# 512-column products with halves added on VectorE in three more stages, and a reordered complex product, in a two-block fp32 model on one core

## The reference

```python
# first block
h = rms_norm(x, norm_ffn_pre)
x = x + rms_norm(conv_ffn(h, ffn_w_up, ffn_conv, ffn_w_down), norm_ffn_post)
# second block, mixer: y_b is the convolution branch
hy = centred_short_conv(hy, conv_w, conv_b)
x0, x1, v = jnp.split(hy, 3, axis=-1)
y_b = x0 * bidirectional_fftconv(v * x1, h_f, h_b, hyena_bias)   # spectrum of u times spectrum of the filter
# second block, experts (peer_ffn)
qh = (xb @ w_q)
s = jnp.einsum('thpc,hpnc->thpn', qh, sk)       # similarities to the sub-keys, then top-16 twice
act = jax.nn.gelu(jnp.einsum('td,thkd->thk', xb, u)) * g
out = jnp.einsum('thk,thkd->td', act, v)
```

## Time and profile before

| | |
|---|---|
| median of 3 runs | 1596.46 us (1592.6 to 1598.15) |
| the profiled execution | 1591.63 us |
| its span, first to last instruction | 1589.8 us |
| TensorE busy | 1551.2 us (98%) |
| GpSimd, VectorE, ScalarE busy | 1193.8, 996.0, 785.7 us |
| mean granted TensorE clock | 0.997 of full |

### The profile page before, as it was taken

The page is one execution under the profiler, slowest core; times in us unless marked ns, Lnnn a source line. Parts: engine busy times, 40 slices in busy tenths (PEclk is TensorE's granted clock), DMA queues, the critical chain, the costliest instruction groups (busy, mean ns, idle before and its releaser), DMA issues.

```text
span 1589.8 us, 30453 instructions
## 1 busy us (share of the span) xinstructions
PE 1551.2 (98%) x11198; PEld 1389.7 (87%) x11198; DVE 996.0 (63%) x1344; ACT 785.7 (49%) x1050; POOL 1193.8 (75%) x499
## 2 busy tenths in 40 slices
PE   7999999999999999999999999999999999999998
PEld 5688899997999889989999999888888888888886
DVE  5545477665220957743159962688888999954444
ACT  5456644556555555444544454454544444444443
POOL 6643689795887964568768998777777777789895
PEclk9999999999999999999999999999999999999999
DMA  8433466555555533336645555555555555566663
GB/s 279 165 111 108 151 219 185 185 184 160 185 184 158 164 113 101 118 124 183 218 144 184 183 180 178 172 167 163 164 167 159 171 160 168 165 221 192 192 194 121
DMA packets 72774, 267.90 MB, mean 169 GB/s; under 512 B 8176, under 2 KB 8448, under 8 KB 71744
## 3 DMA queue, kind: packets, MB, share of 16 engines
q1 hardware_dynamic: 70272, 253.99, 51.0%
q0 software_dynamic: 1568, 7.12, 1.3%
q10 hardware_dynamic: 864, 5.77, 0.9%
HBM read 263.70 MB, written 3.15 MB: 168 GB/s over the span
## 4 chain that ended last, share of the span: by engine, by line
PE 73%; POOL 11%; issue 10%; DVE 3%; ACT 1%; DMA 1%; POOLq 0%; DVEq 0%; SPq 0%; ACTq 0%
PE ps L1132 72%; POOL ring_lo L1192 11%; DMA ring<-in_stream 1%; DVE big L889 1%; ACT ring_hi L1611 0%; DVE hgrn_lo L1851 0%; DMA big<-in_filt 0%; PE ps L1399 0%; DVE big L1877 0%; DVE big L1879 0%; DVE big L1876 0%; DVE h_both L1868 0%; PE ps L1261 0%; DVE big L902 0%; ACT h_both L1624 0%
## 5 line engine op out<-in xcount | busy, mean ns | idle before, releaser
L1192 POOL TENSOR_TENSOR ring_lo<-ring,ring_hi 128x1024 fp32r<-128x1024 f32 x472 | 1172.2, 2500 | 370.4 <-ACT ring_hi L1611 368.7
L1132 PE MATMUL ps<-h_both,ring_hi 128*128 128x256 f32 (+1 forms) x3664 | 749.9, 299 | 2.8 <-DVE h_both L1868 2.7
L1611 ACT CAST ring_hi<-ring 128x1024 fp32r<-128x1024 f32 x472 | 489.8, 1050 | 471.2 <-DMA ring<-in_stream 470.8
L1132 PEld LDWEIGHTS ps<-h_both,ring_hi 128*128 128x128 f32 x3664 | 587.4, 191 | 25.4 <-issue 4.2
L1132 PE MATMUL ps<-h_both,ring_lo 128*128 128x256 f32 x2080 | 585.6, 282 | 0.0
L1132 PE MATMUL ps<-ring_hi,h_both 128*128 128x512 f32 (+1 forms) x1408 | 426.8, 381 | 9.9 <-POOL ring_lo L1192 4.2
L1132 PEld LDWEIGHTS ps<-h_both,ring_lo 128*128 128x128 f32 x2080 | 397.1, 191 | 0.0
L1132 PEld LDWEIGHTS ps<-ring_hi,h_both 128*128 128x128 f32 x1408 | 259.8, 188 | 62.7 <-issue 10.1
L1132 PE MATMUL ps<-ring_lo,h_both 128*128 128x512 f32 (+1 forms) x704 | 265.5, 377 | 0.0
L1851 DVE TENSOR_TENSOR h_both<-big,h_both 128x512 fp32r<-128x512 f32 x64 | 121.2, 1895 | 102.5 <-ACT h_both L1624 102.5
L1132 PEld LDWEIGHTS ps<-ring_lo,h_both 128*128 128x128 f32 x704 | 132.6, 188 | 23.4
(11 more groups left out here) (301 smaller groups left out, 1419.4 us busy)
## 6 DMA issues: line engine op xcount, KB each, us to landing
ring<-in_stream SPq DMA_DIRECT2D x480, 512.0 KB, 3.9
residual<-big ACTq DMA_DIRECT2D x2, 1024.0 KB, 4.0
big<-residual ACTq DMA_DIRECT2D x2, 1024.0 KB, 5.9
x<-in_x SPq DMA_DIRECT2D x2, 512.0 KB, 5.3
big<-in_fdecay POOLq DMA_DIRECT2D x1, 1024.0 KB, 8.9
wrow<-in_post POOLq DMA_DIRECT2D x2, 512.0 KB, 5.5
big<-in_x ACTq DMA_DIRECT2D x1, 1024.0 KB, 5.0
big<-in_subkeys POOLq DMA_DIRECT2D x1, 1024.0 KB, 6.2
```

The source lines that it names most:

```text
L1132: return nc.tensor.matmul(out, lhsT, rhs, start=start, stop=stop, skip_group_check=True)
L1192: P.tensor_tensor(ring_lo[:, h % RING, :], ring[:, h % RING, :], ring_hi[:, h % RING, :].bitcast(fp32), ALU.subtract).then_inc(S["split_lo ...
L1611: A.copy(ring_hi[:, h % RING, :], ring[:, h % RING, :]).then_inc(S["split_hi"], 1)
```

## The change

The wide form of expert slots 32 to 62 is also used for the 22 feed-forward slots, the 12 convolution slots, the 8 query slots and expert slots 25 to 31. Each gets the ScalarE copy of the second halves and the VectorE addition. The waits of TensorE for free banks change accordingly: in the feed-forward, for the finished low part (ffn_gated) of slot i-2; in the convolution slots, for the last tap of slot idx-2, and after slot 11 for the last tap of that slot; in the queries, for the sum of slot s-2. In the feed-forward the GELU is issued on ScalarE behind the first split of the next slot, and the gated product is written to PSUM. Expert slot 0 comes ahead of the first similarities and slot 1 ahead of the second. The first two products with the real spectrum of u are made before the imaginary one is there, and each half of the complex product is finished in turn, through a buffer in PSUM.

```diff
+            def wide_product(n, s, it=None, ready=None):
+                for j in range(2):
+                    bank = 2 * (s % 2) + j
+                    w_hi, w_lo = weights(n, j, it, 6)
+                    for k in range(KC):
+                        if ready and j == 0:
+                            ready(k)
+                        mm(ps[:, bank, :], w_hi[:, tile(k)], h_both[:, :, k, :], k == 0, False)
+                        last = mm(ps[:, bank, 0:SEQ], w_lo[:, tile(k)], h_hi[:, k, :], False, k == KC - 1)
+                    multiplied(last)
...
             for idx in range(12):
-                if idx == 2:
+                if idx == 1:
                     pe.wait_ge(S["spectrum_copied"], 4)
-                channels(idx, ready=None if idx else lambda k: wait_normed(2, k))
+                elif idx >= 2:
+                    pe.wait_ge(S["hy_dve"], 2 * idx - 2)
+                wide_product(W_HY + idx, idx, ready=None if idx else lambda k: wait_normed(2, k))
+            pe.wait_ge(S["hy_dve"], 24)
...
-            pe.wait_ge(S["y_spectrum"], 3)
+            pe.wait_ge(S["y_spectrum"], 2)
...
-            for idx in range(44, 52):
-                channels(idx, ready=None if idx > 44 else lambda k: wait_normed(3, k))
-            pe.wait_ge(S["wq_taken"], 8)
+            for s in range(8):
+                if s < 2:
+                    pe.wait_ge(S["ba_taken"], s + 3)
+                else:
+                    pe.wait_ge(S["columns_summed"], QUERY_SUMS + s - 1)
+                wide_product(W_Q + s, s, ready=None if s else lambda k: wait_normed(3, k))
...
             for t in range(TOK):
+                experts(t)
                 if t:
-                    experts(0)
                     pe.wait_ge(S["sim_copied"], 1)
+                else:
+                    pe.wait_ge(S["columns_summed"], QUERY_SUMS + 8)
...
-            with pe.Fori(0, 3) as it:
-                for s in range(23, 26):
-                    experts(s, it)
+            for s in range(23, FIRST_WIDE):
+                experts(s)
+            for s in range(FIRST_WIDE, 32):
+                wide_experts(s)
...
+                ahead(2 * slot_of(s) + 4)
+                act.wait_ge(S["half_multiplied"], 2 * slot_of(s) + 2)
+                A.copy(XH[:, 2 * s:2 * s + 2, :], ps[:, wide_banks(s), SEQ:2 * SEQ]).then_inc(S["low_products_copied"], 1)
                 ahead(2 * slot_of(s) + 5)
-                act.wait_ge(S["half_multiplied"], 2 * slot_of(s) + 2)
+                act.wait_ge(S["columns_summed"], HY_SUMS + s + 1)
...
-            step(V.tensor_tensor(YT, UI, flat(KI), ALU.mult))
-            step(V.tensor_tensor(flat(YR), UR, flat(KR), ALU.mult))
-            V.tensor_tensor(flat(YR), flat(YR), YT, ALU.add).then_inc(S["y_spectrum"], 1)
-            dve.wait_ge(S["y_spectrum"], 1)
-            step(V.tensor_tensor(flat(YI), UR, flat(KI), ALU.mult))
-            step(V.tensor_tensor(YT, UI, flat(KR), ALU.mult))
-            V.tensor_tensor(flat(YI), flat(YI), YT, ALU.subtract).then_inc(S["y_spectrum"], 1)
-            dve.wait_ge(S["y_spectrum"], 2)
-            for y, parts in ((YR, UR), (YI, UI)):
-                V.tensor_tensor(parts[:, 0:D], y[:, 0, :], y[:, 1, :], ALU.add)
-                last = V.tensor_tensor(parts[:, D:2 * D], y[:, 0, :], y[:, 1, :], ALU.subtract)
-            last.then_inc(S["y_spectrum"], 1)
+            u_part(0, UR)
+            V.tensor_tensor(YR, UR, flat(KR), ALU.mult)
+            step(V.tensor_tensor(YI, UR, flat(KI), ALU.mult))
+            u_part(1, UI)
+            low, high = slice(0, D), slice(D, 2 * D)
+            for y, kernel, parts, op in ((YR, KI, UR, ALU.add), (YI, KR, UI, ALU.subtract)):
+                step(V.tensor_tensor(YT, UI, flat(kernel), ALU.mult))
+                V.tensor_tensor(YT[:, low], y[:, low], YT[:, low], op)
+                step(V.tensor_tensor(y[:, high], y[:, high], YT[:, high], op))
+                V.tensor_tensor(parts[:, low], YT[:, low], y[:, high], ALU.add)
+                V.tensor_tensor(parts[:, high], YT[:, low], y[:, high], ALU.subtract).then_inc(S["y_spectrum"], 1)
...
-                if i >= 4:
-
-                    pe.wait_ge(S["ffn_conv_dve"], at(2 * (i - 3), 8, it))
+                if i >= 2:
+
+                    pe.wait_ge(S["ffn_gated"], at(i - 1, 4, it))
...
                 if it is None:
+                    ahead(first)
+                    if i:
+                        ffn_gelu(i - 1)
                     ahead(2 * n + 5)
                 else:
...
+                A.copy(CONV[:, i % 2], ps[:, wide_banks(i), SEQ:2 * SEQ]).then_inc(S["low_products_copied"], 1)
+                act.wait_ge(S["columns_summed"], at(i + 1, 4, it))
...
+                sums = ps[:, wide_banks(i), 0:SEQ]
+                V.tensor_tensor(sums, sums, CONV[:, i % 2], ALU.add).then_inc(S["columns_summed"], 1)
...
-                V.tensor_tensor(CONV[:, i % 2, 0, :], CONV[:, i % 2, 0, :], CONV[:, i % 2, 1, :],
-                                ALU.mult).then_inc(S["ffn_product"], 1)
+                gated = ps[:, 2 * (i % 2), 0:SEQ]
+                V.tensor_tensor(gated, CONV[:, i % 2, 0, :], CONV[:, i % 2, 1, :], ALU.mult).then_inc(S["ffn_product"], 1)
```

More of the change, by code:

```diff
@@ L505, in gates @@
                 last.then_inc(S["gate_product"], 1)
[L508 to L514, removed]
-                        mm(ps[:, bank, :], w_hi[:, tile(k)], h_both[:, :, k, :], k == 0, False)
-                        last = mm(ps[:, bank, 0:SEQ], w_lo[:, tile(k)], h_hi[:, k, :], False, k == KC - 1)
-                    multiplied(last)
             gates(0)
@@ L734, in activations @@
                              ACT.Gelu_apprx_tanh).then_inc(S["h_ready"], 1)
-            similarities(0)
-            activations(0)
-            similarities(1)
-            for s in range(1, 5):
+            for t in range(TOK):
+                activations(t)
+                similarities(t)
+            for s in range(2, 5):
                 activations(s)
@@ L753, in act_second @@
             A.copy(ROUTE[:, 2, :], ps[:, 5, 0:256]).then_inc(S["routes_copied"], 1)
-            with act.Fori(0, 3) as it:
-                for s in range(23, 26):
-                    activations(s, it)
+            for s in range(23, FIRST_WIDE):
+                activations(s)
             def low_products(s, it=None):
@@ L847, in dve_second, with u_part @@
             flat = lambda a: a.rearrange("p a b -> p (a b)")
-            for part, u in enumerate((UR, UI)):
+            def u_part(part, u):
                 dve.wait_ge(S["u_spectrum_copied"], part + 1)
@@ L990, in dve_second @@
             norm_dve(3, inverse_of_halves)
+            for s in range(8):
+                dve.wait_ge(S["low_products_copied"], QUERY_SUMS + s + 1)
+                queries = QT[:, 2 * s:2 * s + 2, :]
+                V.tensor_tensor(queries, ps[:, wide_banks(s), 0:SEQ], queries, ALU.add).then_inc(S["columns_summed"], 1)
             def best(rows, values, indices, low=-3e38):
@@ L1048, in dve_second, with columns @@
             dve.wait_ge(S["gate_rest"], 1)
+            def columns(s, it=None):
+                dve.wait_ge(S["low_products_copied"], at(EXPERT_SUMS + s - FIRST_WIDE + 1, 6, it))
+                sums = ps[:, wide_banks(s), 0:SEQ]
+                V.tensor_tensor(sums, sums, H[:, bass.ds(at(2 * s, 12, it), 2), :], ALU.add).then_inc(S["columns_summed"], 1)
             def onehots(q, it=None):
@@ L1088, in rest @@
                 rest_of(flat(H[:, bass.ds(at(2 * s, 2 * span, it), 2), :]), flat(h_hi[:, place, :]), flat(h_lo[:, place, :]))
+            for s in range(FIRST_WIDE, 31):
+                columns(s)
             onehots(0)
+            columns(31)
             onehots(1)
@@ L1789, in _, with ffn_gelu @@
             norm_act(1)
+            def ffn_gelu(i, it=None):
+                act.wait_ge(S["ffn_conv_dve"], at(2 * i + 1, 8, it))
+                A.activation(CONV[:, i % 2, 0, :], CONV[:, i % 2, 0, :], ACT.Gelu_apprx_tanh).then_inc(S["ffn_gelu"], 1)
             def ffn_act(i, n, it=None):
+                first = 2 * n + 4 - 2 * (i % 2 == 0)
                 if it is None:
+                    ahead(first)
+                    if i:
+                        ffn_gelu(i - 1)
                     ahead(2 * n + 5)
                 else:
-                    for h in range(2 * n + 4 - 2 * (i % 2 == 0), 2 * n + 6):
+                    split(first, it, 6)
+                    ffn_gelu(i - 1, it)
+                    for h in range(first + 1, 2 * n + 6):
                         split(h, it, 6)
```

66 lines of the change are left out of this document (38 added, 28 removed).

## The result

The changed kernel takes 1598.84 us (median of 20 runs, 1596.83 to 1600.39), the kernel before 1593.74 us (20 runs, 1590.65 to 1598.15). The ratio is 1.0025, with a 95% interval of 1.0018 to 1.0032: 4.0 us slower. I had forecast 1.1 us faster. The profiled execution took 1599.12 us, and its span is 1597.3 us at a mean granted clock of 0.991; the kernel before had 1589.8 us at 0.997. The two profiled executions are so 7.5 us apart, more than the medians: they are good for finding where time goes, not for how much.

A forecast was written before the change was run, and what follows sets the result against it. TensorE, busy for 98% of the span, was taken as the bound. Feed-forward -2.4, convolution +3.9, complex product 0, queries -2.3 and experts -0.3 sum to -1.1 us, so 1595.4 us, range 1586.5 to 1602.5.

The forecast's parts named there:

- -4.6 + 0.15 + 2.1 = -2.4 us: Feed-forward: 4.6 us saved by joined matmuls, 0.15 given back for the first slot, 2.1 of waits, so 2.4 us faster.
- -4.6, the saving of 22 slots: Feed-forward: joined groups take 0.347 us instead of 0.360, 0.21 us saved in each of 22 slots.
- 2.1, the waits in slots 2 and 3: First feed-forward slots, no down product between: TensorE waits 0.9 us for slot 0, 1.2 more for slot 1.
- The chain of copy, split, activations and taps: Convolution channels: 4.5 us per slot, covered by 5.55 between slots, but waited for bare after slot 11.
- The matmul saving of 2.5 us: Convolution channels: joining the matmuls of the 12 slots saves 2.5 us, at 0.21 us a slot.
- what is late next: Second value product: waits 5.4 us for the gated inverse transform (L918), behind ScalarE's decays, instead of 0.32.
- a GpSimd wait would hide the lower clock: After the second value product's wait: the 1.64 us wait for GpSimd at 583.4 hides any lower clock.
- ScalarE's wait for the routes: Queries: similarities 5.0 us later, TensorE would wait about 3 us, but earlier VectorE steps shrink by 4; priced 0, bounds 0 to 3.
- (A): Whole kernel: the sum of the terms holds, 1591.7 to 1600 us; chance 0.56.
- (B): Whole kernel faster: matmul saving kept and covers hold, -4.9 to -10 us, about 1589 us; chance 0.29.
- (C): Feed-forward loop: two-slot look-back becomes the bound from a mean product of 3.4 us; about 1604 us; chance 0.11.
- (D): All converted slots: joining two matmuls saves nothing outside the slots with gates, 1605.7 us; chance 0.04.

## Why the prediction was wrong

The parts, each put back by itself, give against 1.0026:

| part | forecast | measured |
|---|---|---|
| feed-forward | -2.4 us | +1.8 (ratio 1.0015 without it) |
| convolution channels | +3.9 | +4.0 (1.0001) |
| complex product | 0 | 0 (1.0027) |
| queries and experts | -2.6 | -1.9 (1.0038) |
| sum | -1.1 | +3.9 |

Each is good to some 2 us, so that they add up to the whole, 4.1, so closely is partly luck. Of the 5 us between the sums, 4.2 lie in the feed-forward. **The step that failed is its balance, "-4.6 + 0.15 + 2.1 = -2.4 us"**, in three of its terms:

- **-4.6, the saving of 22 slots.** I took the group's 0.347 us from the one stretch where the form already ran. In the convolution of this profile it held (403.12 to 407.97 us is 14 groups, 0.346 each), but in the feed-forward's loop, below, the same 14 groups take 4.95 us, 0.354 each:

```profile
269.36 0.28 PE L1166 MATMUL ps<-h_both,ring_lo 128*128 128x256 f32 x1
...
274.31 0.28 PE L1166 MATMUL ps<-h_both,ring_lo 128*128 128x256 f32 x1
```

  With 18 slots joined and no wait, the stage saved 2.4 us, 0.135 a slot, so 22 are worth 3.0 and not 4.6: 1.6 us.
- **2.1, the waits in slots 2 and 3.** They were 0.80 and 2.25. Slot 1's product (L2158) took 3.83 us beside GpSimd, and I had priced its wait at 1.2 inside bounds of 0 to 3.9: 0.95 us.
- **Nothing for the clock.** I priced a lower clock behind slot 12 and none here, though 2.25 us of waiting is not far from the 3.48 of the earlier trace rows. In every profile of a kernel with this wait a stretch of half clock follows it, and none there in the six without it: 3.4 us at half clock, all of it behind the wait, so 1.7 us.

Together 4.3 us. The stage's own length gives it once more: -3.0 + 3.05 + 1.7 + 0.15 = +1.9, against 2.0 measured.

**Right, by their steps.** The chain of copy, split, activations and taps before slot 12 gave 4.5 us, and TensorE waited 4.2. Wait and clock together were priced at 6.2 us, and taking them out gained 6.1. For the clock I had 1.6. The two profiles of the changed kernel show 6.8 us of half clock there, of which 2.9 and 2.4 us are lost behind the wait, and the medians give about 2. The matmul saving of 2.5 us holds only where the groups take 0.347 us. In seven of the fourteen profiles with joined convolution slots they took 0.353, and it is worth about half. So the 3.9 rests in part on two terms that were off in opposite directions. For the complex product, "what is late next" was named rightly, L918, now L945: 5.4 us forecast, 5.7 waited. That a GpSimd wait would hide the lower clock was right only in its result. That wait went, 6.8 us at half clock came and cost 2.3, and the old form paid as much in the wait of 3.5 us, its 1.7 us of clock and 2.5 us for GpSimd.

**The queries.** The first similarities came later and ScalarE's wait for the routes did not stall TensorE, because the two steps ahead of it shrank as argued, by 4.3 us together: the copy (L1036 before, L1067 now) from 2.32 us to 0.17, the subtraction (L1037, L1068) from 2.57 us to 0.42. They run from 941.63 us on, and GpSimd stands idle from 941.56 to 943.73 us:

```profile
941.84 0.42 DVE L1068 TENSOR_TENSOR aux<-aux,stat 128x256 f32<-128x256 f32 x1
```

**The rivals.** The measured 4 us lie within the 4.8 of (A), with the sum's sign wrong. (B) did not come, since all waits did. (C) did not come, but its point of decision is real: with 5.5 us for product, cast and subtraction instead of 2.6 the loop was bound by the look-back (run with the product in SBUF). (D): joining does save, more than the 2.5 ns a group that follow from the Trainium skill's formula for a single matmul's gap (TensorE: Matmul & The Clock Gate, "Back-to-back issue gap"): 13 ns in the convolution of this profile, 7 in the feed-forward.

## What to carry over

Cheaper matmuls on a full TensorE are worth only what its waits leave: here each new wait of 2 to 6 us brought 3.4 or 6.8 us at half clock as well (only what lies behind the wait costs), so price both wherever a look-back gets shorter, first of all in a stage's first slots and at its last one, and wait for the slot whose bank is taken, not for all. When a wait moves to another name with much the same length (gate, low parts, value copy: 5.7, 5.5, 4.0, 4.6 us), look for the one instruction that they stand behind in an engine's order; here it was ScalarE's copy of the totals, itself waiting for VectorE, and no cover short of the last was worth anything alone. Read a price from more than one stage: a rhythm of TensorE from one loop need not hold in the next.

## What the runs showed of the hardware

- **Joined groups have two steady rhythms**, 0.347 and 0.353 us, each held over tens of slots. The feed-forward loop ran at 0.353 in every profile where its slots did not wait; the convolution's slots ran at 0.347 in some kernels and at 0.353 in others (4.95 us for 14 groups in the run with the old complex product, below), and the experts from slot 32 on changed from the one to the other on the way in both profiles of the changed kernel, where the kernel before held 0.347 throughout. That is 1 to 2 us that the forecast did not have. What chooses is open. VectorE's accesses to PSUM are not enough to explain it: with the product in SBUF groups of 0.353 remained, beside some of 0.347 in slots after a wait.

```profile
403.11 0.28 PE L1165 MATMUL ps<-h_both,ring_lo 128*128 128x256 f32 x1
...
408.06 0.28 PE L1165 MATMUL ps<-h_both,ring_lo 128*128 128x256 f32 x1
```

- **The same wait lowers the clock or not.** The 2.50 us wait near 151 us, in code that is alike in all kernels, was followed by no half clock in two of the other kernels' profiles and in that of before, by 3.4 us in most, and by 6.8 us in three.
- **A 256-element cast on VectorE** took 0.42 us with its input in PSUM and 2.34 us with it in SBUF beside a busy GpSimd; the kernel before had 1.36 us for it. Where GpSimd was idle the kernel before took 0.29 us for the same cast between SBUF buffers, less than the 0.42 from PSUM, and 0.43 us for a product of the same size.

```profile
203.01 0.29 DVE L2114 CAST ffn_hi<-big 128x256 fp32r<-128x256 f32 x1
```

- **The clock can fall while the wait still lasts.** 1.0 and 2.1 us of the half clock at the two long waits lay inside them, and none inside the wait of 3.48 us in the kernel before, where the clock was full until TensorE went on (555.67 us). Counting the whole stretch as loss overstates it.
